# Recurrence units overlapped with the inverse before them, with a second set of buffers on half of the weight ring

## The chip, the cores and the metric

One NeuronCore of one Trainium2 chip runs the whole program in one launch. The metric is device time in microseconds (us) of one execution; the kernel before took 2703.21 us (median of three runs, 2700.9 to 2709.52).

## The reference, cut to what matters

One inference step of a two-layer trunk for 128 context tokens and 256 latent tokens (three tiles of 128 tokens, t = 0, 1, 2), all in fp32. Layer 0 runs grouped-query attention and an RWKV-7 recurrence side by side, layer 1 a gated DeltaNet and differential attention; each layer ends in a mixture of 64 experts. The condition vectors give six modulation sections per layer (`silu(cond) @ mod_w[l] + mod_b[l]`, each 1024 wide); layer 0 needs sections 0 and 1 at its start and sections 2 to 5 after its mixers, layer 1 needs all six only at its start.

The change sits in layer 0's recurrence, which runs forward (d = 0) and backward (d = 1):

```python
def step(S, inp):
    r_t, w_t, k_t, v_t, a_t, b_t = inp
    sa = jnp.einsum('bhij,bhj->bhi', S, a_t)
    S = S * w_t[:, :, None, :] + sa[..., None] * b_t[:, :, None, :] + v_t[..., None] * k_t[:, :, None, :]
    return S, jnp.einsum('bhij,bhj->bhi', S, r_t)
...
w_log = -jax.nn.softplus(-(p['b_w0'][d] + jnp.tanh(wd) @ p['b_w2'][d])) - 0.5
a = jax.nn.sigmoid(p['b_a0'][d] + ad @ p['b_a2'][d])
k_d = kb * (1 + (a - 1) * p['b_ka'])
```

## The kernel before, in words

The kernel gives every engine its own instruction list, written out by hand; semaphores order them, and each engine works strictly in the order of its list. PE (TensorE) multiplies into eight PSUM banks, DVE (VectorE) and ACT (ScalarE) move and combine, SP (SyncE) issues the weight loads. `mm` (L556) is the helper behind nearly every matmul and L1525 the helper `tt` behind most DVE operations, so these two lines stand for many places; shapes tell them apart. One `mm` shows as two hardware instructions in the trace.

Weights pass through a ring of six slots of 1 MB each. SP issues the pieces in a fixed order; `wait_slot_free` (L282) makes each wait until the piece six places earlier has been released. A modulation section is four pieces; `mod_section` (L568) multiplies it on PE (32 `mm`, 64 instructions of form 128*2 128x256), then drains and releases all four slots. `turn_mods` (L582) transposes a finished section.

The recurrence of a tile is computed as one 128-token chunk instead of step by step. A unit is one tile and one direction; `RWKV_UNITS` lists six of them, (0,0), (0,1), (1,0), (2,1), (2,0), (1,1), and `rwkv` runs them one after the other. A unit has these steps on PE (from L734 on):

1. raw gates: two 512-wide products (64*128 64x512), whose sums with the biases DVE forms and whose sigmoids ACT takes;
2. one modulation section while ACT works (units 0 to 3 do a second one a step later);
3. decay sums: two 512-wide products with triangular constants and four narrow ones, whose exponentials ACT takes; DVE then scales the four token arrays;
4. 16 transposes of the tokens (L753), copied out by DVE and ACT;
5. Grams: 16 products 64x256, masked by DVE into the matrix to invert and three others;
6. reads: what the state and the values give (units with t > 0 also read a carried state);
7. the inverse (`invert`, L684): six levels, each two products per head pair and group, between which DVE masks (`join`, L1743, first half) and adds (second half), then the last corner with ACT's copies;
8. solve and outputs, and for units 0 to 3 (`RWKV_KEEPS`) the new state. DVE's sums close the unit (`unit_saved`), and the next unit's raw gates wait for that.

The ten sections that are not needed at the very start, four of layer 0 (`LATE`) and six of layer 1, are spread over the six units (`SECTIONS`): two in each of units 0 to 3, one in units 4 and 5. Layer 0's attention stands before the recurrence; its 24 steps (8 of one key tile, 16 of three) are `scores(u)`, `turn(u - 1)`, `weigh(u - 2)` on PE, with a maximum on DVE and an exponential and a copy on ACT between them.

## Time and profile before

| | |
|---|---|
| median of the runs | 2703.21 us (2700.9 to 2709.52) |
| profiled execution | 2691.1 us, span 2689.2 us, mean granted clock 0.866 |
| PE busy | 2190.0 us (81% of the span) |
| DVE busy | 836.1 us (31%) |
| ACT busy | 355.7 us (13%) |
| attention of layer 0 | about 178 to 252 us after the span's start |
| six recurrence units | 265.4 to 706.9 us |

How to read it: a row of a stretch gives its length and each engine's busy time with its number of instructions, then the granted TensorE clock (1.00 is 2.4 GHz, 0.50 is 1.2 GHz), the busy share of the DMA engines and GB/s. A row of a timeline gives start, duration, engine, line, operation, what is written and read, shapes, how many instructions were merged, and in brackets the engine's idle time before it and who ended it. Matmuls are pipelined and their ends are modelled, so a PE busy share of 1 is not a PE at its peak.

### The profile page before, as it was taken

How to read it: one execution, taken by the hardware profiler on the slowest of the kernel's cores; microseconds unless marked ns; L12 is line 12 of the kernel's file. 1: busy time of each engine (PE TensorE's matmuls, PEld its weight loads, DVE VectorE, ACT ScalarE, POOL GpSimd, SP SyncE). 2: the span in 40 equal slices, each digit the busy share in tenths (PEclk: the TensorE clock that was granted, in tenths of full speed). 3: DMA queues.
4: the chain of work that ended last, by engine and by line, in shares of the span. 5: the costliest groups of instructions: out<-in, count | busy, mean ns of one | idle time of the engine just before them, and what ended most of it. 6: DMA issues, size and time to landing. Idle time of an engine off the chain costs nothing.

```text
span 2689.2 us, 37987 instructions
## 1 busy us (share of the span) xinstructions
PE 2190.0 (81%) x16019; PEld 1506.1 (56%) x16019; DVE 836.1 (31%) x1598; ACT 355.7 (13%) x777; POOL 205.0 (8%) x214
## 2 busy tenths in 40 slices
PE   5968788777699888888893998777699889889883
PEld 2445666666585555555552445476585555555551
DVE  1343433433533111111114263455633111111114
ACT  0012111111011111111110013200011111111110
POOL 0000000000101111111110000000000111111110
PEclk7975988877789999999996997578899999999996
DMA  8450333311035999999997143000005999999996
GB/s 303 129 145 1 127 126 130 127 63 64 26 65 196 384 381 376 381 372 380 369 381 301 63 137 115 0 1 9 6 31 201 392 380 384 371 384 363 372 373 238
DMA packets 129927, 581.36 MB, mean 216 GB/s; under 512 B 25890, under 2 KB 33052, under 8 KB 78424
## 3 DMA queue, kind: packets, MB, share of 16 engines
q1 hardware_dynamic: 88368, 496.07, 47.8%
q0 software_dynamic: 28480, 60.42, 6.7%
q10 hardware_dynamic: 12904, 22.35, 2.8%
q8 instruction: 132, 2.16, 0.3%
q14 instruction: 43, 0.35, 0.0%
HBM read 566.42 MB, written 48.30 MB: 229 GB/s over the span
## 4 chain that ended last, share of the span: by engine, by line
PE 62%; DMA 20%; DVE 11%; issue 3%; PEld 2%; ACT 1%; SPq 1%; PEldq 1%; ACTq 0%; DVEq 0%; POOL 0%; POOLq 0%
PE bank L556 57%; DMA ring<-in_exp_w_up 11%; DVE arena L1525 7%; DMA ring<-in_exp_w_down 3%; DMA ring<-in_mod_w 2%; PEld bank L556 1%; DMA arena<-choice_rows 1%; PE bank L1043 1%; PE bank L660 1%; DMA ring<-in_ev_w_in 1%; DVE mixed L1525 1%; PE bank L1067 1%; DVE arena L1533 1%; PE bank L753 1%; DVE arena L1539 1%
## 5 line engine op out<-in xcount | busy, mean ns | idle before, releaser
L556 PE MATMUL bank<-ring,arena 128*64 128x256 f32 (+3 forms) x5168 | 923.4, 442 | 132.5 <-DMA ring<-in_exp_w_up 87.5
L556 PEld LDWEIGHTS bank<-ring,arena 128*64 128x64 f32 (+1 forms) x5168 | 569.0, 156 | 457.2 <-issue 349.5
L556 PE MATMUL bank<-arena 64*64 64x64 f32 (+8 forms) x6176 | 423.6, 253 | 50.7 <-DVE arena L1525 29.4
L556 PEld LDWEIGHTS bank<-arena 64*64 64x64 f32 (+5 forms) x6176 | 365.3, 159 | 83.4 <-DVE arena L1525 38.8
L1539 DVE COPY arena<-bank 128x512 f32<-128x512 f32 (+3 forms) x253 | 149.1, 605 | 499.5 <-PE bank L556 398.7
L556 PE MATMUL bank<-ring,hT 128*128 128x512 f32 (+2 forms) x672 | 265.5, 555 | 12.3 <-DMA ring<-in_ev_w_in 6.0
L1533 DVE SCALAR_TENSOR_TENSOR arena<-bank,arena 128x256 f32<-128x256 f32 (+1 forms) x84 | 39.9, 476 | 688.6 <-PE bank L556 688.6
L556 PEld LDWEIGHTS bank<-ring,hT 128*128 128x128 f32 x672 | 128.1, 199 | 148.8 <-issue 143.5
L2242 POOL DMA_INDIRECT arena<-token_rows,arena x80 | 90.7, 1134 | 884.7 <-PE bank L1043 563.4
L1525 DVE TENSOR_TENSOR arena<-arena 128x1024 f32<-128x1024 f32 (+7 forms) x135 | 125.1, 949 | 40.5 <-DMA arena<-choice_rows 35.0
L556 PE MATMUL bank<-hT,ring 128*128 128x384 f32 x384 | 130.8, 498 | 1.7 <-ACT hT L1405 1.7
L556 PEld LDWEIGHTS bank<-hT,ring 128*128 128x128 f32 x384 | 106.2, 278 | 23.2 <-issue 4.2
L1043 PE MATMUL bank<-consts,arena 128*128 128x128 f32 x640 | 100.1, 281 | 6.7 <-DVE arena L1539 6.7
L2248 POOL DMA_INDIRECT choice_rows<-arena x80 | 79.8, 997 | 331.5 <-DVE arena L1539 331.5
L1525 DVE TENSOR_TENSOR arena<-bank,consts 128x256 f32<-128x256 f32 (+1 forms) x156 | 74.4, 501 | 82.7 <-PE bank L556 82.7
L1525 DVE TENSOR_TENSOR arena<-arena,bank 128x512 f32<-128x512 f32 (+3 forms) x206 | 89.5, 450 | 33.2 <-PE bank L556 31.7
L556 PE MATMUL bank<-arena,consts 64*64 64x64 f32 (+5 forms) x460 | 72.4, 353 | 26.8 <-DVE arena L1529 12.2
L1043 PEld LDWEIGHTS bank<-consts,arena 128*128 128x128 f32 x640 | 75.7, 144 | 29.2 <-issue 17.7
L1141 ACT ACTIVATE arena<-bank 128x256 f32<-128x256 f32 (+3 forms) x104 | 42.8, 424 | 366.5 <-PE bank L556 366.5
L1471 ACT COPY arena<-bank 128x256 f32<-128x256 f32 x80 | 29.8, 372 | 457.2 <-PE bank L1067 457.2
L556 PE MATMUL bank<-ring,cond 128*2 128x256 f32 x768 | 61.3, 469 | 31.5 <-DMA ring<-in_mod_w 24.4
L2219 POOL MEMSET arena<- 64x256 f32 x18 | 5.5, 307 | 1055.8 <-DVE arena L1525 651.8
(176 smaller groups left out, 1278.7 us busy)
## 6 DMA issues: line engine op xcount, KB each, us to landing
ring<-in_exp_w_gate SPq DMA_DIRECT2D x128, 1024.0 KB, 10.3
ring<-in_exp_w_up SPq DMA_DIRECT2D x128, 1024.0 KB, 9.8
ring<-in_exp_w_down SPq DMA_DIRECT2D x128, 1024.0 KB, 10.1
ring<-in_mod_w SPq DMA_DIRECT2D x48, 1024.0 KB, 9.7
ring<-in_od_w_in SPq DMA_DIRECT2D x14, 1024.0 KB, 9.1
arena<-choice_rows POOLq DMA_DIRECT2D x4, 3072.0 KB, 14.5
ring<-in_ev_w_in SPq DMA_DIRECT2D x10, 1024.0 KB, 16.0
arena<-arena ACTq DMA_DIRECT2D x12, 672.0 KB, 10.8
```

Of the source, the lines that this page charges most:

```text
L556: return nc.tensor.matmul(out, lhsT, rhs, start=start, stop=stop, **kw)
L660: last = nc.tensor.transpose(bank[2 + u % 2][:, k * P:(k + 1) * P], A.p[:, u % 2, k * P:(k + 1) * P], C["ident"])
L753: last = nc.tensor.transpose(bank[b][:, j * P:(j + 1) * P], src[:, j * P:(j + 1) * P], C["ident"])
L1043: last = nc.tensor.transpose(bank[half][:, c * P:(c + 1) * P], g_x[x.b][:, (4 * half + c) * P:(4 * half + c + 1) * P], C["ident"])
L1067: last = nc.tensor.transpose(bank[4][:, c * P:(c + 1) * P], g_h[x.b][:, c::2], C["ident"])
L1141: return nc.scalar.activation(out, in_, func, **kw)
L1471: nc.scalar.copy(g_ht[x.b], heads(bank[4][:, 0:2 * P], 2)).then_inc(sem("ht_saved"), 1)
L1525: return nc.vector.tensor_tensor(out, a, b, op)
L1533: return nc.vector.scalar_tensor_tensor(out=out, in0=a, scalar=s, in1=b, op0=op0, op1=op1)
L1539: return nc.vector.tensor_copy(out, a)
L2242: nc.gpsimd.indirect_dma_start(g_x[x.b], None, x_rows[l], row(x, 0), bounds_check=NTOK - 1, oob_is_err=False).then_inc(sem("expert_loaded" ...
L2248: nc.gpsimd.indirect_dma_start(y_rows[l], row(x, 1), g_y[x.b], None, bounds_check=TOP_K * NTOK - 1, oob_is_err=False).then_inc(sem("scatte ...
```

## The change

The units are no longer run one after the other. Steps 1 to 5 of the next unit stand between the levels of the current unit's inverse, on all three engines; only unit 0's steps 1 to 5 still run by themselves ahead of the first inverse. What the next unit writes while the current one still reads gets a second buffer: the masked matrices, the turned tokens and the two decayed token arrays. Those second buffers lie on ring slots 3 to 5, so while layer 1's sections pass (`narrow`) the ring has three slots, and the first load that goes back to slot 3 (the last piece of layer 0's output projection) waits for the last unit's sums.

The modulation sections move as well. Layer 0's four late sections are multiplied during the attention, one quarter (one piece) behind each of steps 1 to 16, with all six slots; layer 1's six sections go one to a unit, in four parts between the levels, and each half section is released by itself. ACT copies the rows out in the attention loop, and the four late sections are transposed just before unit 0. POOL's clearing of a corner waits for the first level's products instead of for the masked matrix. Layer 1's DeltaNet uses the same level functions in the order it had.

```diff
@@ -64,8 +65,8 @@
 TURNS = 40
 
 EARLY, LATE = (0, 1), (2, 3, 4, 5)
-SECTIONS = [[(0, 2), (0, 3)], [(0, 4), (0, 5)], [(1, 0), (1, 1)], [(1, 2), (1, 3)], [(1, 4)], [(1, 5)]]
-DONE = [sum(len(x) for x in SECTIONS[:u]) for u in range(7)]
+SECTIONS = [(1, s) for s in range(6)]
...
+            for part in ([quarters[0:2], quarters[2:4]] if l else [quarters]):
+                add(part)
 
...
+    narrow = range(starts.pop(0), starts.pop(0))
+    slots = [n % RING if n < narrow[0] else (n - narrow[0]) % NARROW if n in narrow else (n - narrow[-1] - 1) % RING
+             for n in range(len(pieces))]
+    return pieces, group, starts, mods_at, slots, narrow
...
         def wait_slot_free(sp, n):
 
-            m = n - RING
+            m = held_by[n]
+            if m < narrow[0] and n > narrow[-1]:
...
-        (r_ar, r_bt, r_kt, r_tokb, r_tokk, r_toka, r_tokr, r_nr0, r_nr1, r_ak0, r_ak1, *r_inv, r_rs, r_us) = region(
+        (r_ar0, r_bt, r_kt, r_tokb0, r_tokk0, r_toka, r_tokr, r_nr00, r_nr01, r_ak00, r_ak01, *r_inv, r_rs, r_us) = region(
             1024, 512, 512, 512, 512, 512, 512, 1024, 1024, 1024, 1024, *([512] * 8), 512, 512, at=po0)
-        r_ar = r_ar.rearrange("p (c k n) -> p c k n", c=4, k=2)
+
+        wide_ring = ring[:, NARROW:RING, :].rearrange("p s n -> p (s n)")
+        r_nr10, r_nr11, r_ak10, r_ak11, r_ar1 = (wide_ring[:, 1024 * i:1024 * (i + 1)] for i in range(5))
+        r_tokb1, r_tokk1 = (wide_ring[:, 5120 + 512 * i:5632 + 512 * i] for i in range(2))
+        r_tokb, r_tokk = (r_tokb0, r_tokb1), (r_tokk0, r_tokk1)
+        four_pairs = lambda a: a.rearrange("p (c k n) -> p c k n", c=4, k=2)
+        r_ar = [four_pairs(a) for a in (r_ar0, r_ar1)]
         r_bt, r_kt = (a.rearrange("p (c n) -> p c n", c=4) for a in (r_bt, r_kt))
-        r_nr = [a.rearrange("p (c k n) -> p c k n", c=4, k=2) for a in (r_nr0, r_nr1)]
-        r_ak = [a.rearrange("p (c k n) -> p c k n", c=4, k=2) for a in (r_ak0, r_ak1)]
-        r_inverse = Inverse([a[:, :, 0, :] for a in r_nr], r_inv[2:4], r_inv[4:6], r_inv[6:8])
-        r_sig, r_gate, r_ei, r_ev, r_ee, r_x = r_inv[0:6]
+        r_nr = [[four_pairs(a) for a in pair] for pair in ((r_nr00, r_nr01), (r_nr10, r_nr11))]
+        r_ak = [[four_pairs(a) for a in pair] for pair in ((r_ak00, r_ak01), (r_ak10, r_ak11))]
+        r_inverse = [Inverse([a[:, :, 0, :] for a in pair], r_inv[2:4], r_inv[4:6], r_inv[6:8]) for pair in r_nr]
+        r_sig, r_gate = r_inv[0:2]
+        r_ei, r_ev, r_ee = params[:, 0:512], params[:, 1920:2432], params[:, 2432:2944]
         r_rs, r_us = (a.rearrange("p (h d) -> p h d", h=8) for a in (r_rs, r_us))
...
 
+            def mod_part(u, q):
+
+                n = mods_at[SECTIONS[u]] + q
+                if q == 0 and u + 1 < len(RWKV_UNITS):
+                    pe.wait_ge(sem("zw_sum"), u + 2)
+                loaded(n)
+                for c in (2 * q, 2 * q + 1):
+                    four = rows(n, 2, D)[:, c % 2, :].rearrange("p (f r j) -> p r f j", r=4, j=2)
+                    for r in range(4):
+                        mm(bank[5][32 * r:32 * r + 2, 0:256].rearrange("p (f j) -> p f j", j=2), cond[:, c, :],
+                           four[:, r, :, :], c == 0, c == J - 1)
+                if q % 2 == 1:
+                    pe.drain().then_inc(sem("ring_released"), 1)
+                if q == 3:
+                    pe.sem_inc(sem("mod_rows_ready"), 1)
...
+                    if l == 0 and 1 <= u <= 16:
+                        mod_quarter(*divmod(u - 1, 4))
...
+                for u, (t, d) in enumerate(RWKV_UNITS):
+                    inv, v = r_inverse[u % 2], u + 1
+                    more = v < len(RWKV_UNITS)
+                    level_products(inv, u, 0)
+                    if more:
+                        raw_gates(v)
+                    reads(u)
+                    level_joins(inv, u, 0)
+                    mod_part(u, 0)
+                    level_products(inv, u, 1)
+                    mod_part(u, 1)
+                    level_joins(inv, u, 1)
+                    mod_part(u, 2)
+                    level_products(inv, u, 2)
+                    if more:
+                        decay_sums(v)
+                    level_joins(inv, u, 2)
+                    mod_part(u, 3)
+                    level_products(inv, u, 3)
+                    turn_section(u)
+                    level_joins(inv, u, 3)
+                    if more:
+                        turn_tokens(v)
+                    level_products(inv, u, 4)
+                    level_joins(inv, u, 4)
+                    if more:
+                        grams_of_b(v)
+                    level_products(inv, u, 5)
+                    level_joins(inv, u, 5)
+                    if more:
+                        grams_of_k(v)
+                    corner_products(inv, u, (d, d))
+                    corner_joins(inv, u, (d, d))
+                    solve(u)
+                    unit_outputs(u)
...
+                    if l == 0 and u % 4 == 1 and 5 <= u <= 17:
+                        i = u // 4 - 1
+                        save_rows(len(EARLY) + i + 1, next_rows[i], 6 + i % 2)
...
+                for u in range(len(RWKV_UNITS)):
+                    inv, v = r_inverse[u % 2], u + 1
+                    more = v < len(RWKV_UNITS)
+                    mask_products(inv, u, 0)
+                    if more:
+                        gate_inputs(v)
+                    add_joins(inv, u, 0)
+                    mask_products(inv, u, 1)
+                    add_joins(inv, u, 1)
+                    mask_products(inv, u, 2)
+                    if more:
+                        gated_keys(v)
+                    add_joins(inv, u, 2)
+                    mask_products(inv, u, 3)
+                    if more:
+                        decayed_tokens(v)
+                    add_joins(inv, u, 3)
+                    mask_products(inv, u, 4)
+                    if more:
+                        turned(v)
+                    add_joins(inv, u, 4)
+                    mask_products(inv, u, 5)
+                    if more:
+                        masked(v, 0, r_nr)
+                    add_joins(inv, u, 5)
+                    if more:
+                        masked(v, 1, r_ak)
+                    unit_sums(u)
...
                     a, c = inv.corners(dirs[g])
-                    pool.wait_ge(inv.sem("nt_ready", g), n + 1)
```

The order of PE in one step of the attention with three key tiles, before (scores, three transposes, the weighted values; each matmul counted once):

```order
L556 MATMUL bank<-arena 128x384 [waits p_ready]
L660 MATMUL bank<-consts,arena 128x128 [waits pT_saved,p_ready]
L660 MATMUL bank<-consts,arena 128x128 x2
L556 MATMUL bank<-arena 128x64 [waits pT_saved]
L556 MATMUL bank<-arena 128x64 x2
```

and now, in the step where layer 0's fourth section begins (L695 to L719 are the attention, L579 is `mm`):

```order
L579 MATMUL bank<-arena 128x384 [waits p_ready]
L719 MATMUL bank<-consts,arena 128x128 [waits pT_saved,p_ready]
L719 MATMUL bank<-consts,arena 128x128 x2
L579 MATMUL bank<-arena 128x64 [waits pT_saved]
L579 MATMUL bank<-arena 128x64 x2
L579 MATMUL bank<-ring,cond 2x256 [waits ring_loaded_1]
L579 MATMUL bank<-ring,cond 2x256 x7
```

A quarter of a section, eight `mm`, has come in behind each step; the next step's scores stand behind it.

The order of PE in a level of the inverse, before: products of the two groups (x8 each), then their joins (x16 each); the next level's products follow at once:

```order
L556 MATMUL bank0<-arena 64x64 [waits inverse_t_ready_0]
L556 MATMUL bank0<-arena 64x64 x7
L556 MATMUL bank1<-arena 64x64 [waits inverse_t_ready_1]
L556 MATMUL bank1<-arena 64x64 x7
L556 MATMUL bank2<-arena 64x64 [waits inverse_m_saved_0]
L556 MATMUL bank2<-arena 64x64 x15
L556 MATMUL bank3<-arena 64x64 [waits inverse_m_saved_1]
L556 MATMUL bank3<-arena 64x64 x15
```

and now, level 2 of unit 1 (its matrix lies on the ring; banks 4 to 7 are the next unit's):

```order
L579 MATMUL bank0<-arena,ring 64x64 [waits inverse_t_ready_0]
L579 MATMUL bank0<-arena,ring 64x64 x7
L579 MATMUL bank1<-arena,ring 64x64 [waits inverse_t_ready_1]
L579 MATMUL bank1<-arena,ring 64x64 x7
L579 MATMUL bank6<-arena,consts 128x512 [waits read_saved,sig_ready]
L579 MATMUL bank7<-arena,consts 128x512
L579 MATMUL bank4<-consts,arena 128x2 x4
```

The next unit's decay sums have come in between the level's products and its joins; behind the joins stands the fourth quarter of the section.

The order of DVE in the last level of the inverse, before: two masks, then the sums, in three parts for each group:

```order
L1525 TENSOR_TENSOR arena<-bank0,consts 128x256 [waits inverse_m_ready_0]
L1525 TENSOR_TENSOR arena<-bank1,consts 128x256 [waits inverse_m_ready_1]
L1525 TENSOR_TENSOR arena<-arena,bank2 128x256 [waits inverse_join_ready_0]
L1525 TENSOR_TENSOR arena<-arena,bank2 64x4x64 x2
L1525 TENSOR_TENSOR arena<-arena,bank3 128x256 [waits inverse_join_ready_1]
L1525 TENSOR_TENSOR arena<-arena,bank3 64x4x64 x2
```

and now, in unit 1 (L1700 is `tt`; banks 4 to 7 hold the next unit's Grams):

```order
L1700 TENSOR_TENSOR arena<-bank0,consts 128x256 [waits inverse_m_ready_0]
L1700 TENSOR_TENSOR arena<-bank1,consts 128x256 [waits inverse_m_ready_1]
L1700 TENSOR_TENSOR arena<-bank4,consts 128x512 [waits gram_ready]
L1700 TENSOR_TENSOR arena<-bank5,consts 128x512
L1700 TENSOR_TENSOR arena<-bank6,consts 128x512 [waits gram_ready]
L1700 TENSOR_TENSOR arena<-bank7,consts 128x512
L1700 TENSOR_TENSOR arena<-arena,bank2 128x256 [waits inverse_join_ready_0]
L1700 TENSOR_TENSOR arena<-arena,bank2 64x4x64 x2
L1700 TENSOR_TENSOR arena<-arena,bank3 128x256 [waits inverse_join_ready_1]
L1700 TENSOR_TENSOR arena<-arena,bank3 64x4x64 x2
```

Four of the next unit's eight Gram masks stand between the masks and the sums; the other four follow behind the sums. In the same way its bias sums stand in level 0, its three operations for the gated keys in level 2, its four token products in level 3 and two copies in level 4.

## Rows read from the trace of the kernel before

**Rows 1.** Two stretches: from:to, length, busy per engine (instructions), granted clock, DMA.
```profile
178.00:265.40 87.40, 74.00 (x237) 50.78 (x237) 22.98 (x41) 25.23 (x80) 0.00 (x0) 0.52 0.10 27
265.40:706.90 441.50, 353.76 (x5330) 292.96 (x5330) 168.02 (x311) 60.24 (x141) 3.68 (x12) 0.80 0.25 97
```
**Rows 2.** What PE waited for in the units: us in total, times, longest.
```profile
PE bank L556 <- DVE arena L1525: 42.9, 48, 5.0
...
PE bank L556 <- DVE params L1525: 9.0, 4, 2.7
...
PE bank L556 <- DMA ring<-in_mod_w: 8.6, 8, 2.7
```
**Rows 3.** PE's timeline in unit 4: start, duration, what [idle before <- who ended it].
```profile
559.44 2.08 PE L556 MATMUL bank<-hT,arena 64*128 64x512 f32 x4 [2.73 <-DVE params L1525]
561.45 0.93 PE L586 MATMUL bank<-consts,params 98*128 98x98 f32 x4
...
567.35 1.96 PE L556 MATMUL bank<-arena,consts 128*128 128x512 f32 x4 [0.27 <-issue]
569.14 0.95 PE L556 MATMUL bank<-consts,arena 128*128 128x2 f32 x8
574.76 3.53 PE L753 MATMUL bank<-consts,arena 128*128 128x128 f32 x16 [4.67 <-DVE arena L1525]
579.76 3.73 PE L556 MATMUL bank<-arena 64*128 64x256 f32 x32 [1.47 <-DVE arena L1539]
588.45 1.97 PE L556 MATMUL bank<-params,arena 64*128 64x64 f32 x16 [4.96 <-DVE arena L1525]
...
593.96 1.97 PE L556 MATMUL bank<-consts,arena 64*64 64x64 f32 x32
...
599.80 3.09 PE L556 MATMUL bank<-arena 64*64 64x64 f32 x96 [0.33 <-DVE arena L1525]
...
618.40 4.28 PE L556 MATMUL bank<-arena 64*64 64x64 f32 x24 [0.17 <-ACT arena L1313]
623.41 1.98 PE L556 MATMUL bank<-params,arena 64*128 64x64 f32 x16 [0.73 <-ACT arena L1358]
625.32 7.09 PE L556 MATMUL bank<-arena 128*128 128x64 f32 x32
```
**Rows 4.** PE's timeline in units 1 and 3: a quarter, the transposes, the new state.
```profile
343.41 1.10 PE L556 MATMUL bank<-ring,cond 128*2 128x256 f32 x16 [0.22 <-DMA ring<-in_mod_w]
...
347.33 1.94 PE L753 MATMUL bank<-consts,arena 128*128 128x128 f32 x16 [0.26 <-issue]
...
554.74 1.98 PE L556 MATMUL bank<-arena 128*64 128x64 f32 x32
```
**Rows 5.** DVE's timeline in unit 4: tokens, Gram masks, the last level's sums.
```profile
572.21 2.49 DVE L1525 TENSOR_TENSOR arena<-arena 128x512 f32<-128x512 f32 x4
...
583.52 4.87 DVE L1525 TENSOR_TENSOR arena<-bank,consts 128x512 f32<-128x512 f32 x8 [3.91 <-PE bank L556]
...
614.82 2.40 DVE L1525 TENSOR_TENSOR arena<-arena,bank 128x256 f32<-128x256 f32 x6 [0.51 <-PE bank L556]
```
**Rows 6.** The chain that ended last, in the attention: start, us, what.
```profile
192.00 1.04 PE bank L556 x4
193.45 1.04 PE bank L556 x4
...
214.84 2.75 PE bank L556 x8
218.42 2.75 PE bank L556 x8
```
**Rows 7.** PE's timeline at the kernel's start: a quarter of a section.
```profile
17.65 1.89 PE L556 MATMUL bank<-ring,cond 128*2 128x256 f32 x16 [1.17 <-DMA ring<-in_mod_w]
```
**Rows 8.** DMA issues from 105 to 300 us: count, KB each, median us to landing.
```profile
ring<-in_mod_w SPq DMA_DIRECT2D x14, 1024.0 KB, 9.7
```
**Rows 9.** PE's timeline behind the last unit: the output projection's transposes.
```profile
731.40 4.58 PE L882 MATMUL bank<-consts,mixed 128*128 128x128 f32 x24 [19.04 <-DVEq L255]
```

More of the change, by code:

```diff
@@ L59 @@
 RING = 6
+NARROW = 3
 SLOT = 2048
@@ L146, in add_modulation @@
             mods_at[l, s] = len(pieces)
-            add([mod[:, 2 * q:2 * q + 2, s * D:(s + 1) * D] for q in range(4)])
+            quarters = [mod[:, 2 * q:2 * q + 2, s * D:(s + 1) * D] for q in range(4)]
+            for part in ([quarters[0:2], quarters[2:4]] if l else [quarters]):
+                add(part)
     add_modulation(0, EARLY)
@@ L388, in build @@
         r_sw = params[:, 1152:1408].rearrange("p (j v) -> p j v", j=4)
[L389 to L390 removed]
+        r_ec = [params[:, 6016 + 8 * i:6024 + 8 * i].rearrange("p (j h) -> p j h", j=4) for i in range(2)]
+        next_rows = [params[:, 1408 + 256 * i:1664 + 256 * i] for i in range(4)]
         kk_of = lambda t: proj0[:, t, 0:512]
@@ new lines, in _, with level_products @@
+            inverse_halves = (slice(0, 64), slice(64, 128))
+            inverse_blocks = [(h, p) for h in range(4) for p in inverse_halves]
+            def level_products(inv, n, k):
+                t = [half_ident.unsqueeze(1).broadcast_to([P, 4, 64]) if k == 0 else a[:, 0, :, :] for a in inv.both]
+                for g in range(2):
+                    if k:
+                        pe.wait_ge(inv.sem("t_ready", g), LEVELS * n + k)
+                    else:
+                        pe.wait_ge(inv.sem("nt_ready", g), n + 1)
+                    for h, p in inverse_blocks:
+                        last = mm(bank[g][p, 64 * h:64 * h + 64], inv.nt[g][p, h, p], t[g][p, h, :])
+                    last.then_inc(inv.sem("m_ready", g), 1)
@@ new lines, in level_joins @@
+            def level_joins(inv, n, k):
+                tt = [half_ident.unsqueeze(1).broadcast_to([P, 4, 64]) if k == 0 else a[:, 1, :, :] for a in inv.both]
+                for g in range(2):
+                    pe.wait_ge(inv.sem("m_saved", g), LEVELS * n + k + 1)
+                    for h, p in inverse_blocks:
+                        mm(bank[2 + g][p, 64 * h:64 * h + 64], tt[g][p, h, :], inv.m1[g][p, h, :])
+                    for h, p in inverse_blocks:
+                        last = mm(bank[2 + g][p, 256 + 64 * h:320 + 64 * h], inv.m1[g][p, h, :], tt[g][p, h, :])
+                    last.then_inc(inv.sem("join_ready", g), 1)
@@ L765, in rwkv, with grams_of_b, grams_of_k, reads @@
+                def grams_of_b(v):
+                    pe.wait_ge(sem("arT_saved"), v + 1)
+                    pe.wait_ge(sem("bkT_saved"), v + 1)
+                    grams(v, r_bt)
+                def grams_of_k(v):
+                    for g in range(2):
+                        pe.wait_ge(r_inverse[0].sem("nt_ready", g), v + 1)
+                    grams(v, r_kt)
+                def reads(u):
+                    t, d = RWKV_UNITS[u]
                     pe.wait_ge(sem("gram_saved"), 2 * u + 2)
+                    if u:
+                        pe.wait_ge(sem("unit_saved"), u)
@@ L1351, in rwkv @@
+                act.wait_ge(sem("za_ready"), 1)
+                save_late_mods()
+                gates(0)
+                decays(0)
+                turned(0)
+                for u, (t, d) in enumerate(RWKV_UNITS):
+                    v = u + 1
+                    more = v < len(RWKV_UNITS)
                     act.wait_ge(sem("read_ready"), u + 1)
@@ L1811, in rwkv, with unit_sums @@
-                        for i in range(2):
-                            last = tt(two(r_ak[g], i), heads(bank[b + 2 + i][:, :], 2), mask, ALU.mult)
-                        last.then_inc(sem("gram_saved"), 1)
-                    join(r_inverse, u)
+                            last = tt(two(dst[v % 2][g], i), heads(bank[4 + 2 * g + i][:, :], 2), mask, ALU.mult)
+                        last.then_inc(sem("gram_saved") if k else r_inverse[0].sem("nt_ready", g), 1)
+                def unit_sums(u):
+                    t, d = RWKV_UNITS[u]
```

327 lines of the change are left out of this document (186 added, 141 removed).

## The prediction, made before the changed kernel ran

> **What bounds the kernel now.** I read the row of stretches first. The six recurrence units take 441.5 us, PE is busy in 353.8 of them at a mean clock of 0.80, DVE in 168, ACT in 60 [rows 1]. So PE is the bound with 87.7 us of holes, and the question is which holes an overlap can fill, and what it puts on PE elsewhere. The waits say who made the holes: DVE's arena operations 42.9 us, the end of a unit (DVE on `params`) 9.0, the mod sections' DMA 8.6 [rows 2]. The longest is the same in each unit: before the reads PE stands 4.96 us for the Gram masks (the row at 588.45) [rows 3]. The timeline of unit 4 then shows what the inverse is like inside: a level is 96 instructions in 3.09 us with 0.33 idle ahead of it (at 599.80) [rows 3]. The reader should see here that the inverse has next to no room on PE. Work put between its levels is added, not hidden; what is gained is the holes of steps 1 to 5, not their PE time.
>
> Last the attention. The stretch from 178 to 265 runs at clock 0.52 [rows 1], and in the chain its steps follow each other on PE alone: 1.45 us each with one key tile (193.45 - 192.00, of which 1.04 is PE), 3.58 with three (218.42 - 214.84) [rows 6].
>
> **The recurrence.** A middle unit of the changed kernel, in PE time from unit 4's rows [rows 3]: raw gates 2.01 (561.45 - 559.44), one section turned 0.47 (half of 0.93, which is two), decay sums 2.74, Grams 3.73, reads 5.51 (593.96 - 588.45), levels with corner and solve 29.45 (623.41 - 593.96, its waits included), outputs 9.00 (to 632.41). With four quarters of a section at 1.10 and the transposes at 1.94 [rows 4] that is 59.3.
>
> New waits. DVE's four token products, 2.49, stand between level 3's masks and sums; four Gram masks, 2.44 (half of 4.87), stand ahead of the last level's sums, 2.40 [rows 5]. Behind them on DVE wait the sums, and PE's next products wait for those. Beside them PE has the joins (64 of 96 instructions, 2.06) and half the Grams (1.87). What sticks out is 0.5 to 1 at three places. Bounds: nothing, and all of it with the copies, 8.6 a unit; I take 2, since PE's cover is near the same length. A unit is then 61.3. Units 2 and 3 add 1.98 for the state [rows 4]: 63.2. Units 0 and 1 have no carried state: 3.8 less (1.90 in the reads, 1.91 in the outputs), 1.98 more: 59.4. Unit 5 prepares nothing and has no new waits: 59.3 - 2.0 - 2.7 - 1.9 - 3.7 = 48.9. Sum: 2 x 59.4 + 2 x 63.2 + 61.3 + 48.9 = 355.4.
>
> Unit 0's preparation stays alone. Unit 4's took 29.0 from gates to reads; 2.4 of it, the second half of the masks, now runs beside the first products: 26.6. So the units take 382, not 441.5: **60 us less**. Bounds -45 (waits of 5 a unit) and -75 (preparation 5 shorter, and no new waits).
>
> **The attention.** Four sections, 16 quarters, come in. At this clock a quarter is 1.89 [rows 7]. With three key tiles PE's chain is closed, so eight quarters cost 8 x 1.89 = 15.1; with one tile 0.41 of each step is not PE and takes part of it: 8 x (1.89 - 0.41) = 11.8. **27 us more.** No row shows a quarter between attention steps, so bounds: 30 (nothing hidden, 16 x 1.89), and a small gain, worked out below. I take 27, since the rows on both sides are at the lower clock. The first six pieces arrive while DVE prepares the keys; later ones are released a section at a time, two steps or more before they are due, and a landing of 9.7 [rows 8] is about three such steps with the quarters in; a late one costs 1 to 3 us, once.
>
> Here a rule of the Trainium skill speaks: "Trainium Kernel Development and Optimization", section "Performance Expectations", holds matmul busy time a bad measure, because matmuls are pipelined; by it PE's full share in the attention need not mean that no room is left, and with all quarters hidden the sum would be -60. No row here decides it; the chain with PE at every step speaks against.
>
> **The small parts.** The second-half load of a section now follows its release with three slots: a landing of 9.7 [rows 8] against some 9 us of PE work until the fourth part; costs 0 to 1 a unit, taken as nothing. The wait of the output projection's fourth piece for the last sums has three loads queued behind it on SP; PE needs them only after 731, with 19.04 of its own idle in front [rows 9]; without that cover it would be 9.7. The row copies moved into ACT's attention loop (four, on an engine busy for 25 of 87 us [rows 1]), POOL's later clearing (needed at the solve, a whole inverse later) and one more DVE clearing at the start lie beside other work: nothing, and some tenths each without cover.
>
> **Sum.** -60 + 27 = -33. The profiled execution took 2691.1 and would take 2658. The median of the runs, 2703.2, lies 12 above it; I put the change on that: **2670**.
>
> **Rivals.**
> *The clock rises.* A quarter is dense work, and the gaps in which PE stood idle go. At the higher clock a quarter is 1.10 [rows 4], and 16 transposes take 1.94 instead of 3.53 [rows 3, 4], a factor of 0.55. Steps with one tile then take 1.04 x 0.55 + 1.10 = 1.67, with three 3.58 x 0.55 + 1.10 = 3.07: 8 x 0.22 - 8 x 0.51 = -2 instead of +27, and up to -15 if the last eight steps stay there too. That gives 2628 to 2641. For it: dense quarters lifted nothing so far only where gaps of a us lay between them [rows 7]. Against: the attention is without gaps and yet low, so being busy alone does not lift it. The Trainium skill, "TensorE: Matmul & The Clock Gate", section "Why this matters for your kernels", says that continuous work releases the clock and gaps take it back; the full attention at 0.52 does not agree.
>
> *The clock falls in the levels: slower.* Levels run at 1.00 today, but their first 32 instructions, straight behind the reads, took 1.97 (at 593.96) [rows 3], 62 ns each against 32. If the inserted transposes and waits hold the clock down, a level costs 96 x 0.030 = 2.8 more; five levels in five units make +71, and the kernel takes 2741. It is slower than before from 12 of these 25 levels on. Against: in unit 1 a quarter and the transposes kept the higher rate (1.10 and 1.94) with waits for DMA between them [rows 4], and the waits that I expect are no longer than those.
>
> *The overlap is spent in order.* If DVE's inserted work comes out in full (8.6 a unit instead of 2, five units: +33), the attention's price eats the rest: 2703, no change. The change then doesn't do what it says: units overlap on paper, and PE waits at each level. DVE's total, 168 in 382, speaks against it; its strict order for it.
>
> **How the numbers follow.** My case (2658 to 2685) has a chance of 0.6, the rise of the clock 0.17, the spent overlap 0.14, the fall 0.09. A measurement of this kernel can tell about 0.3%, 8 us, from no change. Faster: all of my case, the rise, and a fifth of the spent overlap, 0.8; same 0.1; slower 0.1. The range leaves out the deepest end of the rise and the fall: 2636 to 2702.
>
> **What would show it.** Right: the units' stretch falls to about 382 us with PE busy in over 85% of it, the 4.96 wait before the reads is gone, units 1 to 4 take 59 to 63; the attention's stretch grows by 25 to 30 at a clock of 0.5, with 1.89 per quarter. Wrong: waits of PE on DVE above 5 us in a unit (spent overlap); a granted clock clearly below 1 in levels 2 to 5 (fall); quarters of 1.10 in the attention (rise); PE waiting for `mod_w` anywhere; or the output projection starting late behind the last unit.

## The result, and the profile after

The changed kernel takes 2591.7 us (median of 4 runs, 2582.8 to 2609.5), the kernel before 2702.2 (2700.9 to 2709.5): ratio 0.9595, 95% interval 0.9564 to 0.9626. The forecast was 2670 with a range from 2636 to 2702, so the direction was right and the gain three times as large as forecast. The profiled execution took 2592.4, with a span of 2590.6 and a mean granted clock of 0.894 (before 0.866).

The same stretches as in [rows 1], after the change: from:to, length, busy time of PE, PE's weight loads, DVE, ACT and POOL (instructions), granted clock, DMA share, GB/s. The third is the rest of the kernel.

```profile
178.00:260.00 82.00, 65.82 (x499) 37.96 (x497) 24.41 (x41) 26.32 (x84) 0.00 (x0) 0.83 0.54 196
260.00:597.40 337.40, 306.83 (x5069) 258.10 (x5068) 165.03 (x311) 59.70 (x138) 3.69 (x12) 0.87 0.21 77
597.40:2590.00 1992.60, 1633.22 (x10014) 1099.95 (x10014) 588.26 (x1168) 258.48 (x533) 195.96 (x194) 0.90 0.67 252
```

and the rest of the kernel before:

```profile
706.90:2689.00 1982.10, 1633.07 (x10016) 1099.41 (x10016) 588.13 (x1168) 258.56 (x534) 195.68 (x194) 0.90 0.66 252
```

Against [rows 1] the attention's stretch went from 87.4 to 82.0 (forecast +27), the units from 441.5 to 337.4 (forecast -60, measured -104). That is 109.5 us, and the medians differ by 110.5. The last stretch reads 10.5 us longer after the change. That is not the change's doing: to the ends of their spans the changed kernel took 1993.2 there, and two kernels below that have the code of before there took 1994.1 (span 2702.8, outputs of the last unit done at 708.7) and 1989.8 (2672.8 less 683.0). The profiled execution of before (1982.3 to the end of its span), 11 us under its median, was a quick one there. Of the miss of 66 us in the profiled time, then, 45 lie in the units, 32 in the attention, and 11 of the opposite sign in the rest.

PE's timeline in the attention shows why it did not grow (start, duration, what; the rows of 128x256 are quarters, 16 instructions each):

```profile
186.78 1.89 PE L579 MATMUL bank<-ring,cond 128*2 128x256 f32 x16
...
193.32 1.89 PE L579 MATMUL bank<-ring,cond 128*2 128x256 f32 x16
...
196.59 1.25 PE L579 MATMUL bank<-ring,cond 128*2 128x256 f32 x16
...
198.93 1.10 PE L579 MATMUL bank<-ring,cond 128*2 128x256 f32 x16
...
200.80 1.10 PE L579 MATMUL bank<-ring,cond 128*2 128x256 f32 x16
...
209.86 1.10 PE L579 MATMUL bank<-ring,cond 128*2 128x256 f32 x16 [1.32 <-ACT params L1319]
...
215.78 1.10 PE L579 MATMUL bank<-ring,cond 128*2 128x256 f32 x16
...
218.74 1.10 PE L579 MATMUL bank<-ring,cond 128*2 128x256 f32 x16
...
237.31 1.62 PE L579 MATMUL bank<-arena 128*128 128x64 f32 x8
...
239.24 1.62 PE L579 MATMUL bank<-arena 128*128 128x64 f32 x8
```

Three quarters take 1.89 as forecast [rows 7]; the clock rises inside the fourth and stays up for the last 50 us, 16 of them without any quarter. A step with three key tiles takes 2.96 with a quarter in it (218.74 - 215.78) and 1.93 without (239.24 - 237.31), where it took 3.58 without one before [rows 6].

PE's timeline in unit 4, which answers to [rows 3]:

```profile
499.33 1.82 PE L579 MATMUL bank<-hT,arena 64*128 64x512 f32 x4
500.99 1.00 PE L579 MATMUL bank<-params,arena 64*128 64x64 f32 x16
501.92 2.00 PE L579 MATMUL bank<-arena 128*128 128x64 f32 x16
503.85 0.68 PE L579 MATMUL bank<-arena,consts 64*64 64x64 f32 x16
...
513.29 1.98 PE L579 MATMUL bank<-arena,consts 128*128 128x512 f32 x4
515.11 0.95 PE L579 MATMUL bank<-consts,arena 128*128 128x2 f32 x8
515.99 2.08 PE L579 MATMUL bank<-arena 64*64 64x64 f32 x64
...
523.43 1.09 PE L832 MATMUL bank<-consts,arena 128*128 128x128 f32 x8 [0.50 <-DVE ring L1700]
...
534.63 2.00 PE L579 MATMUL bank<-ring,arena 64*128 64x256 f32 x16 [0.87 <-DVE ring L1700]
536.56 4.28 PE L579 MATMUL bank<-arena 64*64 64x64 f32 x48
541.57 1.86 PE L579 MATMUL bank<-params,arena 64*128 64x64 f32 x16 [0.74 <-ACT arena L1534]
543.37 7.09 PE L579 MATMUL bank<-arena 128*128 128x64 f32 x32
```

The wait of 4.96 ahead of the reads is gone, as forecast. But the reads themselves, the same 32 matmuls, take 2.86 (503.85 - 500.99) instead of 5.51. The solve, which stands behind the corner, is shorter too: 48 instructions in 4.28 (at 536.56), where 24 took 4.28 before (at 618.40 in [rows 3]). The outputs at the unit's end are as slow as before (7.09 for 32 matmuls in both): there the clock falls still. What PE waited for in the units:

```profile
PE bank L579 <- DVE arena L1700: 7.0, 8, 2.6
PE bank L832 <- DVE arena L1700: 5.3, 3, 4.3
PE bank L579 <- ACT arena L1534: 4.4, 6, 0.7
```

DVE's 42.9 us in 48 waits [rows 2] have become 7.0 in 8; the mod sections' DMA is gone from the list.

### The profile page after: what moved, and what is told of

Same layout as the page of the kernel before. It is cut to its first block, busy times and chain, and to the rows that moved or that the text cites. A ratio compares the mean times of both kernels' runs of the same rounds, so it can differ in the third digit from the quotient of the medians.

```text
span 2590.6 us, 38020 instructions
## 1 busy us (share of the span) xinstructions
PE 2135.2 (82%) x16019; PEld 1459.3 (56%) x16019; DVE 834.8 (32%) x1599; ACT 356.1 (14%) x777; POOL 205.3 (8%) x214
## 4 chain that ended last, share of the span: by engine, by line
PE 63%; DMA 20%; DVE 10%; issue 3%; PEld 2%; ACT 1%; PEldq 1%; SPq 1%; ACTq 0%; DVEq 0%; POOL 0%; POOLq 0%
PE bank L579 58%; DMA ring<-in_exp_w_up 12%; DVE arena L1700 6%; DMA ring<-in_exp_w_down 3%; PEld bank L579 1%; DMA ring<-in_mod_w 1%; DMA arena<-choice_rows 1%; PE bank L1193 1%; DVE mixed L1700 1%; PE bank L1217 1%; PE bank L719 1%; DVE arena L1708 1%; DVE stats L1711 1%; PE bank L832 1%; SPq L316 0%
## 5 line engine op out<-in xcount | busy, mean ns | idle before, releaser
L579 PE MATMUL bank<-ring,arena 128*64 128x256 f32 (+4 forms) x5264 | 930.8, 438 | 146.2 <-DMA ring<-in_exp_w_up 88.5
L579 PEld LDWEIGHTS bank<-ring,arena 128*64 128x64 f32 (+2 forms) x5264 | 575.0, 156 | 470.5 <-issue 364.3
L579 PE MATMUL bank<-arena 64*64 64x64 f32 (+9 forms) x5344 | 328.8, 242 | 27.6 <-DVE arena L1700 10.6
L579 PEld LDWEIGHTS bank<-arena 64*64 64x64 f32 (+5 forms) x5344 | 278.1, 150 | 72.2 <-issue 46.3
L579 PE MATMUL bank<-ring,hT 128*128 128x512 f32 (+2 forms) x672 | 265.3, 554 | 13.9 <-DVE hT L1705 10.9
L579 PEld LDWEIGHTS bank<-ring,hT 128*128 128x128 f32 x672 | 127.6, 199 | 150.7 <-issue 144.1
L579 PE MATMUL bank<-hT,ring 128*128 128x384 f32 x384 | 130.9, 498 | 1.7 <-issue 0.8
L1700 DVE TENSOR_TENSOR arena<-arena 128x1152 bf16<-128x1152 bf16 (+5 forms) x111 | 110.2, 1006 | 38.0 <-DMA arena<-choice_rows 35.2
L579 PEld LDWEIGHTS bank<-hT,ring 128*128 128x128 f32 x384 | 106.1, 278 | 23.5 <-issue 4.5
L1700 DVE TENSOR_TENSOR arena<-arena,bank 128x512 f32<-128x512 f32 (+3 forms) x206 | 88.6, 449 | 38.2 <-PE bank L579 36.7
L579 PE MATMUL bank<-arena,consts 64*64 64x64 f32 (+5 forms) x460 | 70.7, 337 | 28.7 <-DVE arena L1704 12.2
L1291 ACT ACTIVATE arena<-bank 128x256 f32<-128x256 f32 (+2 forms) x86 | 33.4, 388 | 365.1 <-PE bank L579 365.1
L1652 ACT COPY arena<-bank 128x512 f32<-128x512 f32 x80 | 46.9, 586 | 261.6 <-PE bank L579 261.6
L579 PE MATMUL bank<-ring,cond 128*2 128x256 f32 x768 | 61.7, 446 | 24.9 <-DMA ring<-in_mod_w 16.5
```

Source lines behind the costliest of these rows:

```text
L579: return nc.tensor.matmul(out, lhsT, rhs, start=start, stop=stop, **kw)
L1291: return nc.scalar.activation(out, in_, func, **kw)
L1652: nc.scalar.copy(g_y[x.b][:, 0:512], bank[5][:, :]).then_inc(sem("slots_saved_a"), 1)
L1700: return nc.vector.tensor_tensor(out, a, b, op)
```

## The experiments

A "useless quarter" in what follows is 16 matmuls of the shape of a real one, on constants, into a bank that nobody reads at that time:

```diff
+def idle_quarter(b):
+    four = consts[:, 0:D].rearrange("p (f r j) -> p r f j", r=4, j=2)
+    for c in range(2):
+        for r in range(4):
+            mm(bank[b][32 * r:32 * r + 2, 0:256]..., cond[:, c, :], four[:, r, :, :])
```

The theory: PE's durations are not the instructions' own. Holes and thin work let the granted clock fall to 1.2 GHz and dense work brings it to 2.4, so the change, which fills holes, made instructions faster that it did not touch. The rivals: the attention is faster for another reason (its loads, what stood before it); PE in the units is faster through other banks or buffers, or only its holes went.

**Useless quarters in the attention of the kernel before.**

```diff
                     if u >= 2:
                         weigh(u - 2)
+                    if l == 0 and 1 <= u <= 16:
+                        idle_quarter(7)
```

> The kernel before, with 16 useless quarters (the same 16 matmuls each as a quarter of a section, on constants, into a bank that nobody reads) at the places in the attention where the changed kernel has its 16 real ones. Theory, the clock: dense quarters raise the granted clock in the attention, whatever they compute; the attention gets shorter although PE has 16 quarters more: quarters of 1.10 us from the fourth or so, steps with three tiles near 1.95 behind them instead of 3.58, stretch from 178 to 265 shorter by 5 to 10 us, total 2692 to 2697. Rival, as predicted: the clock stays at 0.5, quarters of 1.89, stretch longer by 27, total 2729. Rival, the rise came from elsewhere in the change: the same 2729.

Ratio to the kernel before 0.9965, interval 0.9942 to 0.9989 (2698.1 us): 16 quarters of pure extra work cost nothing and gained 9 us in the median, which the interval only just sets apart from nothing. The forecast's price of +27 is out. PE's timeline:

```profile
215.39 1.88 PE L556 MATMUL bank<-consts,cond 128*2 128x256 f32 x16
...
219.55 1.10 PE L556 MATMUL bank<-consts,cond 128*2 128x256 f32 x16
...
241.50 1.62 PE L556 MATMUL bank<-arena 128*128 128x64 f32 x8
```

The clock rises at 217 us here, 20 us later than in the changed kernel, and steps then take 1.93 as there (243.43 - 241.50). In this execution the attention ended where it ended without the quarters, so the profile doesn't show where the 9 us come from. It shows quarters that raise the clock; when they do so is not fixed.

**The quarters of the changed kernel in one block behind the attention.**

```diff
-                    if l == 0 and 1 <= u <= 16:
-                        mod_quarter(*divmod(u - 1, 4))
+                if l == 0:                      # behind the loop; ACT's copies too
+                    for k in range(16):
+                        mod_quarter(*divmod(k, 4))
```

> The changed kernel, with its 16 quarters in one block behind the attention instead of between its steps. Theory, the clock: the attention is at 0.5 again, steps with three tiles at 3.58, and the block adds 16 x 1.10 to 1.89: 30 to 43 us longer than the changed kernel, total 2622 to 2635. Rival, the rise has another cause (the time before the attention, the loads): steps stay near 1.95, the block costs what the quarters cost in the steps, total 2588 to 2596.

Ratio 0.9750 (0.9724 to 0.9777), 2634.8 us: 43 us over the changed kernel. The attention and the block:

```profile
178.00:254.60 76.60, 71.19 (x229) 49.16 (x227) 13.73 (x31) 23.33 (x75) 0.00 (x0) 0.50 0.11 31
254.60:291.00 36.40, 25.36 (x257) 6.54 (x256) 0.90 (x2) 1.12 (x3) 0.00 (x0) 0.62 0.75 289
```

The attention is at 0.50 from end to end, with PE busy in 71 of 76.6 us, and longer without its quarters (to 254.6) than with them (to 248). The block is 36 us, 11 of them waits for the pieces, which the attention had covered; so 43 is not the clock's alone. Both runs together settle the first question: the quarters' dense work raised the clock, and a PE that is busy nearly all the time with the attention's own matmuls does not. The other profiles of this document agree: in all ten with quarters between the steps of this attention the clock is up in the later steps, in none of the three without (the kernel before, this run and the next).

**Useless quarters in the holes of the units of the kernel before.**

```diff
                     if u:
+                        idle_quarter(0); idle_quarter(0)
                         pe.wait_ge(sem("unit_saved"), u)
...
+                    else:                       # units 4, 5: ahead of the transposes
+                        for _ in range(4): idle_quarter(0)
...
+                    pe.wait_ge(sem("gram_saved"), 2 * u + 1)
+                    for _ in range(2): idle_quarter(4)
                     pe.wait_ge(sem("gram_saved"), 2 * u + 2)
```

> The kernel before, with useless quarters in PE's holes of the recurrence: two ahead of a unit's raw gates, four ahead of the token transposes in units 4 and 5, two ahead of the reads between the two halves of the Gram masks. Theory, the clock: with the hole filled the reads behind it run at the higher clock (5.51 to about 3, first level 0.6 to 1 less), the raw gates too (2.08 to 1.1): 2 to 4 us a unit, total 2680 to 2692. Rival, PE's durations depend on the instructions and not on what stood ahead: the fillers fit their holes or stick out by some tenths, total 2702 to 2710.

Ratio 0.9857 (0.9830 to 0.9884), 2668.8 us: 38 us faster, more than expected, and nothing in this kernel does less than before. PE's timeline in unit 4:

```profile
575.91 3.20 PE L556 MATMUL bank<-consts,cond 128*2 128x256 f32 x32 [2.57 <-DVE arena L1541]
579.04 1.46 PE L556 MATMUL bank<-params,arena 64*128 64x64 f32 x16
580.44 2.00 PE L556 MATMUL bank<-arena 128*128 128x64 f32 x16
...
608.38 1.11 PE L556 MATMUL bank<-params,arena 64*128 64x64 f32 x16 [0.74 <-ACT arena L1374]
609.42 6.09 PE L556 MATMUL bank<-arena 128*128 128x64 f32 x32
```

The clock rises inside the useless quarters (the first takes 1.9, the second 1.3), and the reads behind them take 3.3 instead of 5.5 [rows 3]. In the units the clock went from 0.80 to 0.87, the changed kernel's figure. Their stretch took 416.6 us in this profile (266.36 to 683.0) for 441.5, so 25 of the 38 us are seen there.

**The changed kernel with its units one after the other.**

```diff
-                grams_of_k(0)  # and the other four of unit 0, ahead of the loop
                 for u, (t, d) in enumerate(RWKV_UNITS):
+                    raw_gates(u); decay_sums(u); turn_tokens(u)
+                    grams_of_b(u); grams_of_k(u)
                     level_products(inv, u, 0)
-                    if more:
-                        raw_gates(v)  # so for the five, and on ACT and DVE
```

> The changed kernel with its buffers, banks and attention, but the units one after the other: a unit's gates, tokens and Grams stand ahead of its own inverse again, on PE, ACT and DVE; the quarters stay between the levels. Theory, the clock: the holes come back (about 55 us) and with them the lower clock behind them, PE busy in the units 20 to 25 us more than the changed kernel's 307 and mean clock near 0.8: total 2660 to 2680. Rival, PE is faster in the changed kernel because of banks, buffers or the place of the quarters: only the holes come back, PE busy stays near 307 and the clock near 0.9, total 2640 to 2650.

Ratio 1.0053 (1.0026 to 1.0080), 2721.6 us: slower than the kernel before, and some 50 us beyond what the theory expected. The units:

```profile
260.00:741.00 481.00, 367.47 (x5070) 301.54 (x5068) 167.94 (x310) 60.18 (x138) 3.68 (x12) 0.72 0.15 54
```

```profile
584.25 3.61 PE L579 MATMUL bank<-arena,consts 128*128 128x512 f32 x4 [3.52 <-ACT arena L1280]
...
593.32 3.68 PE L832 MATMUL bank<-consts,arena 128*128 128x128 f32 x16 [4.67 <-DVE arena L1682]
```

This is the cleanest row of the study. The matmuls are the changed kernel's (5070 against 5069), with its banks and buffers, in another order. The overlap is worth 144 us (481.0 - 337.4): 83 in holes (113.5 against 30.6) and 61 in PE's busy time (367.5 against 306.8), at a clock of 0.72 against 0.87. Decay sums take 3.61 for 1.98, transposes 3.68 for 1.90 (525.33 - 523.43). How much of the 61 is the clock can be estimated from the two traces: 1242 of the matmuls here start at half clock, 613 in the changed kernel; with the changed kernel's mean time for each shape at each of the two levels, this order would be busy for 357 us. So about 50 of the 61 are the clock, and 10 stay unexplained. The rival of banks and buffers is out. The kernel before did better in turn (441.5), I think because its quarters stood in the holes and not between the levels, which my expectation had forgotten; its decay sums came 0.27 behind a section and took 1.96 [rows 3], here 3.52 behind the gates. No run moves the quarters alone.

**Useless quarters in layer 1's attention.** The changed kernel has half clock there as well, so the theory must pay in a place that the change never touched.

```diff
+                    if l == 1 and u % 2 == 1:
+                        idle_quarter(7)
```

> The changed kernel, with a useless quarter (16 matmuls on constants into a bank that nobody reads) behind every second step of layer 1's attention, twelve in all. In the changed kernel that attention starts at full clock and falls to half after its sixth step, 71 us at half. Theory, the clock: dense quarters between the steps hold the clock that is there; steps with three tiles take 2.04 instead of 3.69, 35 us gained, 13 spent: 20 us faster than the changed kernel, ratio to the kernel before near 0.952. Rival, every second step is too thin and the clock falls all the same: 12 x 1.89 added, ratio near 0.968.

Ratio 0.9524 (0.9473 to 0.9575), the theory's number. That attention in the changed kernel, and here:

```profile
1550.00:1624.00 74.00, 70.58 (x216) 46.59 (x216) 18.62 (x49) 21.69 (x72) 0.00 (x0) 0.52 0.07 23
```

```profile
1545.00:1605.00 60.00, 55.41 (x420) 31.40 (x420) 23.21 (x54) 21.38 (x72) 0.00 (x0) 0.93 0.02 7
```

Twice the matmuls in 14 us less, at 0.93 instead of 0.52; the medians differ by some 20, and the rest is not located. The expectation had one thing wrong: in the changed kernel this attention is at half clock from its first steps on, so there was no full clock to hold. Here it starts at half too, and the quarters raise it after the second:

```profile
1550.58 1.89 PE L579 MATMUL bank<-consts,cond 128*2 128x256 f32 x16
...
1554.64 1.10 PE L579 MATMUL bank<-consts,cond 128*2 128x256 f32 x16
```

**Eight of the 16 quarters ahead of the attention.**

```diff
+                if l == 0:                      # ahead of the transposes; four more behind them
+                    for q in range(4): mod_quarter(0, q)
...
-                    if l == 0 and 1 <= u <= 16:
-                        mod_quarter(*divmod(u - 1, 4))
+                    if l == 0 and u % 2 == 1 and u < 16:
+                        mod_quarter(*divmod(8 + u // 2, 4))
```

> The changed kernel, with eight of its 16 attention quarters moved into PE's holes ahead of the attention: four at 160 us, where PE stands idle for 17 us, four behind the transposes, where it stands for 4; the other eight stand at every second step. Theory, the clock: eight quarters leave the steps (11 us), the first steps are at full clock (2 us), and the clock holds with a quarter at every second step: 10 to 13 us faster than the changed kernel, ratio near 0.955. Rival, it takes a quarter at every step: the clock falls again, steps with three tiles at 3.58, 5 to 15 us slower than the changed kernel, ratio 0.962 to 0.965.

Ratio 0.9680 (0.9629 to 0.9730): 20 us slower than the changed kernel, and not only for the rival's reason. PE's timeline:

```profile
179.02 6.27 PE L579 MATMUL bank<-ring,cond 128*2 128x256 f32 x64 [18.14 <-DVEq L269]
...
193.09 1.10 PE L579 MATMUL bank<-ring,cond 128*2 128x256 f32 x16 [3.76 <-DMA ring<-in_mod_w]
195.62 1.89 PE L579 MATMUL bank<-ring,cond 128*2 128x256 f32 x16 [1.43 <-DMA ring<-in_mod_w]
```

The hole at 160 us is the end of a phase, where PE waits for DVE before it starts anything of the next; my quarters stood behind that wait, so they delayed the transposes by 6 us and then waited for pieces. The quarters ahead did raise the clock (1.10 at 193.09), but behind the waits of 3.76 and 1.43 it was down again before the first step (1.89 at 195.62), and it rose once more only at 232 us, with a quarter at every second step. How much of the 20 us is the delay and how much the clock, the run does not part.

**Unit 0's quarters in its own preparation.**

```diff
                 raw_gates(0)
+                mod_part(0, 0); mod_part(0, 1)  # into bank 3; not between unit 0's levels
                 decay_sums(0)
+                mod_part(0, 2)
                 turn_tokens(0)
+                mod_part(0, 3)
```

> The changed kernel, with the four quarters of unit 0 in the holes of that unit's own preparation (28.5 us, 12 of them idle, clock 0.62) instead of between its levels. Theory: the quarters cost nothing there (4.4 us less in the levels), and what follows them runs at the higher clock (decay sums 2.7 instead of 5.5, transposes 1.9 instead of 3.6): 6 to 9 us faster than the changed kernel, ratio near 0.9565. Rival, the holes are gained but not the clock: 4 us, ratio 0.958; or the late landing of the fourth quarter holds up the Grams: no gain.

Ratio 0.9596 (0.9557 to 0.9636): no gain. The preparation took 24.3 us instead of 28.4 (from 275.95 to 300.26), but the attention, the same code as in the changed kernel, ended 16 us later in this execution: it began 2 us later, and its clock rose only in the quarter at 234 us:

```profile
233.88 1.83 PE L579 MATMUL bank<-ring,cond 128*2 128x256 f32 x16
237.90 1.10 PE L579 MATMUL bank<-ring,cond 128*2 128x256 f32 x16
```

**All three of these together.** The edits are the last three diffs.

> The changed kernel with the edits of the last three together. Theory, the clock: they lie in three stretches that do not touch, so the gains add: 36 to 42 us faster than the changed kernel, ratio to the kernel before 0.944 to 0.947. Rival: what one stretch gains at the clock another gives back, ratio above 0.950.

Ratio 0.9547 (0.9483 to 0.9612): above 0.950, as the rival said. The forecast sum does not come out, since of the three one had gained nothing by itself and one had lost 20 us.

**The changed kernel once more,** without an edit, to see whether the moment of the rise belongs to the code.

> The changed kernel once more, for the profile of a second execution. Theory, the clock rises in the attention when dense work has stood there for some steps: the moment is near the fourth quarter again and the raw gates start within 2 us of 260.05; ratio to the kernel before 0.957 to 0.963. Rival: the moment differs from execution to execution of the same code (in the runs whose attention is the same as the changed kernel's it lay at 195 and, in the one with the quarters in the preparation, at 234); then the attention is up to 16 us longer in this profile, and that much of the spread of the times is the attention's.

Ratio 0.9583 (0.9554 to 0.9612), in the first range; but the profile bears out the rival. The quarters of this execution:

```profile
191.33 1.19 PE L579 MATMUL bank<-ring,cond 128*2 128x256 f32 x16
...
208.31 1.63 PE L579 MATMUL bank<-ring,cond 128*2 128x256 f32 x16 [1.31 <-ACT params L1319]
...
213.45 1.88 PE L579 MATMUL bank<-ring,cond 128*2 128x256 f32 x16
...
228.18 1.10 PE L579 MATMUL bank<-ring,cond 128*2 128x256 f32 x16
```

The clock rose at 191, fell near 208, about a wait of 1.31 us for one of ACT's row copies, and rose again near 225. The wait alone is not the cause: the first execution has it too, 1.32 at 209.86, and its clock stayed up. The raw gates came at 266.2 instead of 260.05. The same code, another 6 us, 1 of them from ahead of the first step.

**Useless quarters ahead of the attention.** Twelve ahead of the end of the projection's phase this time, and three behind the transposes.

```diff
+                if l == 0:                      # projection, ahead of end_phase()
+                    for _ in range(12): idle_quarter(7)
...
+                if l == 0:                      # attend, behind the transposes
+                    for _ in range(3): idle_quarter(7)
```

> The changed kernel, with useless quarters in PE's holes ahead of the attention: twelve (13 us) behind layer 0's projection, where PE stands idle for 17 us, and three (3.3 us) behind the attention's transposes, where it stands for 4.0; its own 16 quarters stay in the steps. Theory, the clock: the attention starts at full clock and the real quarters hold it; the first three quarters at 1.10 instead of 1.89 and the first steps at full clock, 4 to 6 us against the profile of the changed kernel, and up to 16 against executions whose clock rises late: ratio 0.953 to 0.958. Rival: the three quarters behind the transposes run at half clock and hold up the first step by 2 us, and nothing else moves: ratio 0.960.

Ratio 0.9552 (0.9527 to 0.9576), 2581.5 us against 2598.6 for the changed kernel on the same chip. The three quarters ahead of the first step, and the first real one:

```profile
180.57 3.69 PE L579 MATMUL bank<-consts,cond 128*2 128x256 f32 x48
...
186.84 1.10 PE L579 MATMUL bank<-ring,cond 128*2 128x256 f32 x16
```

All 16 real quarters take 1.10, and the raw gates come at 255.06, 5 and 11 us earlier than in the two executions of the changed kernel. The 17 us between the medians are not clear of the noise (0.9552 and 0.9583, with intervals that overlap); what the profiles show is 5 to 11.

**A version that beats both.** The last edit, with the quarters in layer 1's attention (three more ahead of it), and unit 0's quarters in the preparation.

> The last one, with the useless quarters behind every second step of layer 1's attention, three ahead of that attention, and unit 0's quarters in its own preparation. Theory, the clock: the gains add, 20 us from layer 1, 4 to 8 from ahead of the attention, 4 to 8 from the preparation: ratio to the kernel before 0.944 to 0.950. Rival, what one stretch gains another gives back: 0.952 or more.

Ratio 0.9472 (0.9449 to 0.9495), 2568.0 us: 30 us below the changed kernel on the same chip (2598.6), in the theory's range. Layer 1 and the quarters ahead of the first attention would account for it, by the medians of their own runs (some 20 and 17 us, the second not clear of the noise); that the preparation adds anything is not shown.

## Why the prediction was wrong

**The direction and the overlap itself** were right. PE's idle time in the units fell from 87.7 to 30.6, PE is busy in 91% of the stretch (over 85% was said), the wait before the reads is gone, and all of PE's idle time is 3 us a unit. "The overlap is spent in order" did not happen, nor did "the clock falls in the levels": they run at 1.10 per quarter and 2.08 for the 64 instructions of a level's joins.

**The step that failed** is "in PE time from unit 4's rows": durations of before were carried over as if they were the instructions' own. The rows from which they came (reads 5.51, raw gates 2.01) stood behind holes that the same text removed. In unit 4, forecast 61.3 and measured 53.0, the reads are 2.65 shorter, the first level 1.0, corner and solve 1.6, the gates 0.35; that is 5.6 of 8.3. The run with the units in turn shows that it is the clock in the main: 61 us on the same matmuls, about 50 of them by the clock's two levels.

**A second, smaller term** went the same way: 29.45 for levels, corner and solve had "its waits included", 0.25 to 0.54 at each level [rows 3]. The inserted work fills those too: 2.4 a unit. The new waits on DVE were sized well, 1.4 measured (0.50 and 0.87) for 2. Over the six units 355.4 was forecast and 308.9 measured; unit 0's preparation, 26.6 forecast, took 28.4.

**The attention** went by "The clock rises", which had a chance of 0.17 and a size of -2 to -15; measured -5.4. That it was a gain at all is partly luck of the execution: in the second one of the same kernel the stretch took 88.2 (178.0 to 266.2), 0.8 more than before. Neither comes near +27. The sentence that kept it low, "being busy alone does not lift it", is true (0.50 with PE busy in 71 of 76.6 us, in the second run) but was no argument against the quarters, which are other work. The rule of the Trainium skill named there, "TensorE: Matmul & The Clock Gate", section "Why this matters for your kernels", that gaps take the clock back, agrees with the units in turn (0.72 against 0.87); that continuous work releases it does not cover the attention's own matmuls. And the rival was priced for the attention alone: the clock of the units was taken as given, in the very part where holes were to vanish. The range's lower end, 2636, fell with that.

One reading in the attention's price was wrong by itself. With one key tile "0.41 of each step is not PE", but the chain has a transpose of PE's there, between the rows of 1.04 that [rows 6] shows:

```profile
193.05 0.40 PE bank L660
```

So at half clock nothing of a step was free for the quarters, and the price should have been the bound of 30; with the quarter, a one-tile step at full clock takes 1.87 (200.80 - 198.93), where the rival said 1.67.

**The small parts** cost nothing, as said: the output projection's transposes come 18.41 us after the last of PE's work, for 19.04 before [rows 9], and PE waits for pieces in the attention for under 1 us in all.

## What to carry to other kernels

A duration read in a profile belongs to the clock of its stretch: before carrying it over, look at the granted clock there and at what stood ahead of it, and ask whether the change removes that. Where a change fills PE's holes, price the instructions behind them at both levels; here the clock was about 50 of the overlap's 144 us. Where a PE-bound stretch reads a clock near 0.5, a few useless dense matmuls are a cheap test of what the clock is worth, and at times a gain.

## What the runs showed of the hardware that was not expected

- Extra work can shorten a kernel: useless quarters in the holes of the units gained 38 us (0.9857), twelve in an attention about 20 (0.9524 against 0.9595; 14 of them seen in that attention).
- PE may be busy almost without a hole and stay at half clock: 76.6 us at 0.50 with 71.2 busy, 4 of the rest in one hole ahead of the first step. Layer 1's attention, at 0.52 by itself, ran at 0.93 with a quarter at every second step.
- The moment at which the clock rises differs between executions of the same attention code: 191, 197 and 234 us; from the first scores to the raw gates that attention took 80, 75 and 89 us. With useless quarters right ahead of the first step the clock was up from the first real quarter on, in both profiles that have them; with real quarters there that waited for their pieces it was down again at the first step (the run with eight quarters ahead). What decides the moment stays open.
